# GpSimd forms the low words of four weight slots of each expert pass in place of two

## The chip, the cores and the metric

The kernel runs on one core of one Trainium2 chip. The metric is the device time in microseconds (us) of one execution; smaller is better.

## The reference

One decoder layer on 1024 tokens of width 1024: a mixer (recurrent branch, sliding-window attention, cross-attention into 256 memory tokens, output projection, residual), then a mixture of experts. The mixer is untouched here. The part that the change lies in is this, cut down:

```python
logits = xt @ w_router + b_router                 # 1024 tokens, 32 experts
top_vals, top_idx = lax.top_k(logits, 4)
gates = softmax(top_vals)
# for each expert, on the tokens that chose it:
h = x_tokens @ w1[e] + b1[e]                      # 1024 -> 2048
x_glu = minimum(h[..., ::2], 7);  x_lin = clip(h[..., 1::2], -7, 7)
a = x_glu * sigmoid(1.702 * x_glu) * (x_lin + 1)
out[tokens] += (a @ w2[e] + b2[e]) * gate         # 1024 -> 1024
```

## The kernel before

All is float32. A matmul takes its operands in a rounded form, so each operand is split into a high word (the rounded value) and a low word (the value minus the high word), and a product is made of three matmuls, high by high, high by low, low by high (`three`, L1030 to L1032).

The experts run in *passes* (a hardware loop, one program for each engine). A pass is one expert on up to 256 tokens, in one or two groups of 128; I call passes with one group single and with two groups double. The weights of a pass come in 12 *slots* of 1 MB: 0 to 7 hold the first matrix (two slots for each of four quarters j of the hidden width), 8 to 11 the second. For every slot:

- SyncE loads it into `ring` (6 places). A load waits until the low words of the slot six before it are made, and these waits stand in slot order.
- ScalarE makes the high words `w_hi` (L712) into one of 4 places (`SPLIT`). It waits until TensorE has used the slot four before (`w_used`).
- VectorE, or for the slots in `BY_POOL` GpSimd, makes the low words `w_lo` = `ring` - `w_hi` (VectorE L1461, a helper that also makes `xT_lo` and `actT_lo`; GpSimd L501), and tells TensorE and SyncE by a semaphore (`lo_ready` for VectorE, `lo_pool` for GpSimd).
- TensorE uses it: 12 matmuls of 128x512 for each group.

The order of an engine's work in a pass is written out by hand. VectorE runs `split_lo(3)`, `split_lo(4)`, then for j = 0 to 3: `add_bias(j)` (for each group `hb` L1524 from PSUM, `glu` L1530, `lin` L1531, and `lin` L1535), for j = 0 the index of the next pass (`make_idx`, L1455 and L1457, which waits for GpSimd's `idx_cur` L505), `split_lo(2j+5)`, for j = 3 `take_xlo` (`xT_lo` of the next pass's group 0), `times_sigmoid(j)` (`act` L1544), for j > 0 `take_alo(j-1)` (`actT_lo`), `split_lo(2j+6)`, and for j = 1 `make_onehot` (L1449). Slots 12, 13, 14 are slots 0, 1, 2 of the next pass. `split_lo` returns at once for a slot in `BY_POOL`. After the four quarters come `take_alo(3)`, slots 13 and 14, `combine` and the `xT_lo` of group 1.

ScalarE runs `split_hi(3)`, `split_hi(4)`, and then for each j: `split_hi(2j+5)`, `sigmoid(j)` (L721), for j = 3 `take_xhi` (`xT_hi`, L687), for j > 0 `take_ahi(j-1)` (`actT_hi`, L727), `split_hi(2j+6)`. `add_bias(j)` waits for TensorE to be done with slot 2j+1.

GpSimd runs in each pass: copy `idx_cur`, two indirect DMAs `xg` (L480) that fetch the next pass's tokens, one DMA `rows` (L514) for each group that fetches the rows of `out`, then the low words of its slots in order, then one DMA `out` (L522) for each group that writes the rows back; at the pass's end it waits for these to land before the next pass's `idx_cur`.

TensorE's slot 9 writes the PSUM bank in which the transposed tokens of the next pass lie, so `down(9)` waits for `xT_lo` of group 0 (`xlo_ready`).

Of the kernel before, what the change touches and what calls it, by code (L numbers as in the profile page):

```python
# [50 lines left out]
RAW = 6  # L51
SPLIT = 4
LEAD = 3
BY_POOL = (7, 11)
AHEAD_OOB = 1 << 20


# [12 lines left out]
def hymba_layer(nc, x, mem, g_mix, w_in, conv_w, conv_b, lru_wa, lru_ba, lru_wx, lru_bx, lru_lambda,  # L70
# [3 lines left out]
    with ExitStack() as ctx:  # L74
# [199 lines left out]
        def split_before(s, by_pool):  # L274

            return sum((i % NSLOT in BY_POOL) == by_pool for i in range(s + 1))

# [22 lines left out]
        def _(sp):  # L300
# [57 lines left out]
            with sp.Fori(0, total) as p:  # L358
# [3 lines left out]

                sp.reg_mul(split_reg, p, NSLOT - len(BY_POOL))
                sp.reg_mul(pool_reg, p, len(BY_POOL))
                for s in range(RAW, RAW + NSLOT):

                    if (s - RAW) % NSLOT in BY_POOL:
                        sp.reg_add(pool_reg, pool_reg, 1)
# [16 lines left out]
        def _(po):  # L385
# [105 lines left out]
            with po.Fori(0, total) as p:  # L491
# [6 lines left out]
                def body(groups):  # L498
                    def split_lo(s):
                        po.wait_ge(hi_ready, p12 + (s + 1))  # L500
                        po.tensor_tensor(w_lo[s % SPLIT][:, :, :], slot(s), w_hi[s % SPLIT][:, :, :].bitcast(F32),  # L501
                                         ALU.subtract).then_inc(lo_pool, 1)
# [9 lines left out]
                    for g in groups:  # L512
# [3 lines left out]
                                              bounds_check=last_row, oob_is_err=False).then_inc(rows_in[g], 16)  # L516
                    for s in BY_POOL:
                        split_lo(s)
# [234 lines left out]
        def _(pe):  # L753
# [285 lines left out]
            with pe.Fori(0, total) as p:  # L1039
                two = pe.value_load(ttab[0:1, bass.ds(p + TTWO, 1)], min_val=0, max_val=1)  # L1040
                dbl = pe.value_load(ttab[0:1, bass.ds(p + TDBL, 1)], min_val=0, max_val=NPASS)
                p_dve, p_pool = pe.snap(p * (NSLOT - len(BY_POOL))), pe.snap(p * len(BY_POOL))

# [578 lines left out]
```

## Time and profile before

| what | us |
|---|---|
| device time, median of 3 runs | 2646.74 (2640.09 to 2650.44) |
| span of the profiled execution, first to last instruction | 2640.5 |
| TensorE matmul busy | 2244.2 (85%) |
| VectorE busy | 1864.1 (71%) |
| ScalarE busy | 1157.0 (44%) |
| GpSimd busy | 638.1 (24%) |

The profiled execution's device time is not listed apart from its span; the span lies 6.2 us under the median of the runs and within their spread. The mixer and the routing take the first 638 us of the span, the 32 passes the rest. The shares are means over all of it. The passes are of few kinds, and passes of one kind are alike, so the change is read in one pass of a kind, in order of time, and multiplied.

### The profile page before, as it was taken

Reading aid. Unit: us, or ns where it says so; the run is one execution under the profiler, and the core shown is the slowest. Engines: PE = TensorE matmul, PEld = TensorE weight load, DVE = VectorE, ACT = ScalarE, POOL = GpSimd, SP = SyncE. Lnnn points to the kernel's source line nnn. Section 1 sums busy time; section 2 is a strip of 40 time slices with the busy share of each in tenths; the row PEclk is TensorE's granted clock in tenths of the full one; section 3 lists DMA queues with packets and bytes.
Section 4 is the critical chain, followed back from the end, with each engine's and each line's share of the span. In section 5 each row is a group of like instructions: output and inputs, shape, how many; then the busy total and the mean of one; then the engine's idle time right before and its main releaser. Section 6 shows DMA issues by size and latency. Waiting matters only on the chain.

```text
span 2640.5 us, 31740 instructions
## 1 busy us (share of the span) xinstructions
PE 2244.2 (85%) x9880; PEld 1699.7 (64%) x9881; DVE 1864.1 (71%) x2162; ACT 1157.0 (44%) x1253; POOL 638.1 (24%) x309
## 2 busy tenths in 40 slices
PE   6998788987699867987798989896777998998996
PEld 4453576444577755766676767675566786786784
DVE  4023773337887887888778888888787778778777
ACT  3025341113444544455444545454554445445444
POOL 1002000002222232223323232323223223223222
PEclk9998997987999977988898989998888998998998
DMA  6001001006776677667767676767777667667665
GB/s 220 0 1 64 25 1 72 32 26 245 268 250 221 230 257 277 232 241 255 267 221 274 226 271 230 245 235 250 265 244 263 219 216 281 216 206 276 215 206 200
DMA packets 244998, 524.29 MB, mean 199 GB/s; under 512 B 17576, under 2 KB 22760, under 8 KB 240737
## 3 DMA queue, kind: packets, MB, share of 16 engines
q1 hardware_dynamic: 220990, 467.84, 50.8%
q0 software_dynamic: 23904, 55.95, 5.6%
q8 instruction: 23, 0.38, 0.1%
q14 instruction: 15, 0.11, 0.0%
q10 hardware_dynamic: 66, 0.02, 0.0%
HBM read 522.20 MB, written 32.11 MB: 210 GB/s over the span
## 4 chain that ended last, share of the span: by engine, by line
PE 45%; DVE 20%; issue 11%; DMA 3%; DVEq 3%; ACT 2%; POOLq 0%; POOL 0%; ACTq 0%
PE ps L1030 12%; PE ps L1032 12%; PE ps L1031 12%; DVE w_lo L1461 5%; PE ps L955 5%; DVE glu L1530 3%; DMA out<-rows,idx_cur 3%; DVE lin L1531 3%; DVE hb L1524 2%; DVE onehot L1449 2%; DVE xT_lo L1461 2%; DVE lin L1535 1%; PE ps L1065 1%; ACT w_hi L712 1%; ACT xT_hi L687 1%
## 5 line engine op out<-in xcount | busy, mean ns | idle before, releaser
L712 ACT ACTIVATE w_hi<-ring 128x2048 fp32r<-128x2048 f32 x384 | 731.2, 1914 | 365.8 <-PE ps L1032 365.5
L1461 DVE TENSOR_TENSOR w_lo<-ring,w_hi 128x2048 fp32r<-128x2048 f32 x323 | 736.5, 2285 | 97.7 <-ACT w_hi L712 93.3
L1030 PE MATMUL ps<-w_hi,xT_hi 128*128 128x512 f32 x1440 | 585.7, 407 | 6.9 <-DVE xT_lo L1461 6.9
L1032 PE MATMUL ps<-w_hi,xT_lo 128*128 128x512 f32 x1440 | 574.8, 399 | 0.0
L1031 PE MATMUL ps<-w_lo,xT_hi 128*128 128x512 f32 x1440 | 574.7, 399 | 0.0
L1030 PE MATMUL ps<-w_hi,actT_hi 128*128 128x512 f32 x720 | 321.5, 447 | 203.6 <-DVE xT_lo L1461 159.8
L501 POOL TENSOR_TENSOR w_lo<-ring,w_hi 128x2048 fp32r<-128x2048 f32 x64 | 316.6, 4947 | 445.6 <-ACT w_hi L712 445.1
L1030 PEld LDWEIGHTS ps<-w_hi,xT_hi 128*128 128x128 f32 x1440 | 280.2, 195 | 63.4 <-issue 7.1
L1032 PEld LDWEIGHTS ps<-w_hi,xT_lo 128*128 128x128 f32 x1440 | 278.6, 193 | 61.4
L1031 PEld LDWEIGHTS ps<-w_lo,xT_hi 128*128 128x128 f32 x1440 | 279.8, 194 | 56.9
L1030 PEld LDWEIGHTS ps<-w_hi,actT_hi 128*128 128x128 f32 x720 | 150.0, 208 | 250.3 <-DVE xT_lo L1461 168.6
L1032 PE MATMUL ps<-w_hi,actT_lo 128*128 128x512 f32 x720 | 305.5, 424 | 0.0
L1031 PE MATMUL ps<-w_lo,actT_hi 128*128 128x512 f32 x720 | 304.4, 423 | 0.0
L522 POOL DMA_INDIRECT out<-rows,idx_cur x45 | 82.2, 1826 | 650.2 <-DVE rows L1561 644.8
L721 ACT ACTIVATE sig<-glu 128x256 f32<-128x256 f32 x180 | 72.7, 414 | 366.4 <-DVE glu L1530 366.1
L727 ACT ACTIVATE actT_hi<-ps 128x256 fp32r<-128x256 f32 x180 | 62.8, 379 | 274.0 <-PE ps L1065 274.0
L1032 PEld LDWEIGHTS ps<-w_hi,actT_lo 128*128 128x128 f32 x720 | 148.8, 207 | 35.3
L1031 PEld LDWEIGHTS ps<-w_lo,actT_hi 128*128 128x128 f32 x720 | 150.7, 209 | 28.3
L1531 DVE TENSOR_SCALAR lin<-hb 128x256 f32<-128x256 f32 x180 | 166.4, 925 | 0.0
L1544 DVE TENSOR_TENSOR act<-lin,sig 128x256 f32<-128x256 f32 x180 | 164.5, 937 | 2.0
L1524 DVE TENSOR_TENSOR hb<-ps,b1b 128x512 f32<-128x512 f32 x180 | 123.1, 684 | 49.4 <-PE ps L1032 49.4
L480 POOL DMA_INDIRECT xg<-token_rows,idx_next x66 | 124.9, 1892 | 105.2 <-issue 79.7
(260 smaller groups left out, 2356.9 us busy)
## 6 DMA issues: line engine op xcount, KB each, us to landing
ring<-in_w SPq DMA_DIRECT2D x390, 1024.0 KB, 5.1
b1b<-in_b SPq DMA_DIRECT2D x33, 1024.0 KB, 6.7
xh<-in_x SPq DMA_DIRECT2D x2, 2048.0 KB, 17.3
work<-in_w_out SPq DMA_DIRECT2D x1, 4096.0 KB, 12.8
token_rows<-uT POOLq DMA_DIRECT2D x8, 512.0 KB, 2.9
out<-xh SPq DMA_DIRECT2D x8, 512.0 KB, 2.6
work<-in_w_in SPq DMA_DIRECT2D x2, 1536.0 KB, 19.8
uT<-in_w_mem_kv SPq DMA_DIRECT2D x1, 2048.0 KB, 17.5
```

What stands on the lines that cost most here:

```text
L480: po.indirect_dma_start(out=xg[:, g, :], out_offset=None, in_=xrows[:, :], in_offset=by_index(idx_next, g), bounds_check=last_row, oob_is_ ...
L501: po.tensor_tensor(w_lo[s % SPLIT][:, :, :], slot(s), w_hi[s % SPLIT][:, :, :].bitcast(F32), ALU.subtract).then_inc(lo_pool, 1)
L522: po.indirect_dma_start(out=out[0], out_offset=by_index(idx_cur, g), in_=rows[:, g, :], in_offset=None, bounds_check=last_row, oob_is_err= ...
L712: act_e.activation(w_hi[s % SPLIT][:, :, :], slot(s), ACT.Copy).then_inc(hi_ready, 1)
L955: m = pe.matmul(ps[:, 2 * g + half, :], uT[:, c, i * P:(i + 1) * P], w_out_sb[:, kk + n, half * HALF:(half + 1) * HALF], start=n == 0, sto ...
L1030: pe.matmul(acc, hi, whi, start=first, stop=False)
L1031: pe.matmul(acc, hi, wlo, start=False, stop=False)
L1032: return pe.matmul(acc, lo, whi, start=False, stop=last)
L1461: return dve.tensor_tensor(lo, x, hi.bitcast(F32), ALU.subtract)
L1524: dve.tensor_tensor(hj, ps[:, 2 * (j % 2) + g, :], b1b[:, j * HALF:(j + 1) * HALF], ALU.add).then_inc(h_free[g], 1)
L1531: dve.tensor_scalar(lin[:, g, j % 2, :], pair[:, 1, :], LIMIT, -LIMIT, ALU.min, ALU.max).then_inc(lin_ready[g], 1)
L1544: dve.tensor_tensor(act[:, g, j % 2, :], lin[:, g, j % 2, :], sig[:, g, j % 2, :], ALU.mult).then_inc(act_ready[g], 1)
```

## The change

`BY_POOL` goes from two slots to four. From it follow, without other edits, the slots that `split_lo` of VectorE skips, the loop of GpSimd, the counts that TensorE and SyncE wait for on the two semaphores (`p * len(BY_POOL)`, `p * (NSLOT - len(BY_POOL))`), and which semaphore each waits on for slots 5 and 9.

```diff
-BY_POOL = (7, 11)
+BY_POOL = (5, 7, 9, 11)
```

## Rows read from the trace of the kernel before

**Rows 1.** Windows, three passes: us; busy (x) PE, PEld, DVE, ACT, POOL; PEclk, DMA, GB/s.

```profile
1379.66:1432.29 52.63, 41.04 (x171) 32.69 (x171) 46.08 (x43) 29.01 (x24) 16.51 (x7) 0.87 0.79 283
1248.20:1306.20 58.00, 42.62 (x171) 33.83 (x171) 46.12 (x42) 29.05 (x24) 18.81 (x7) 0.85 0.75 267
1432.29:1505.80 73.51, 71.63 (x352) 58.83 (x351) 56.30 (x69) 32.96 (x33) 20.16 (x10) 0.98 0.64 221
```

**Rows 2.** Timeline of TensorE at slot 9, in the first single and the double pass.

```profile
1416.82 0.79 PE L1030 MATMUL ps<-w_hi,actT_hi 128*128 128x512 f32 x1 [7.46 <-DVE xT_lo L1461]
...
1483.01 0.50 PE L1030 MATMUL ps<-w_hi,actT_hi 128*128 128x512 f32 x1 [1.88 <-DVE xT_lo L1461]
```

**Rows 3.** Timeline of VectorE in the first single pass, start and duration in us.

```profile
1392.87 5.37 DVE L1544 TENSOR_TENSOR act<-lin,sig 128x256 f32<-128x256 f32 x1
...
1407.36 2.28 DVE L1461 TENSOR_TENSOR w_lo<-ring,w_hi 128x2048 fp32r<-128x2048 f32 x1
1409.56 0.68 DVE L1524 TENSOR_TENSOR hb<-ps,b1b 128x512 f32<-128x512 f32 x1
1410.28 3.87 DVE L1530 TENSOR_SCALAR glu<-hb 128x256 f32<-128x256 f32 x1
...
1415.54 1.23 DVE L1461 TENSOR_TENSOR xT_lo<-ps,xT_hi 128x1024 fp32r<-128x1024 f32 x1 [0.73 <-ACT xT_hi L687]
```

**Rows 4.** Groups by line: count, busy us, mean ns of one, idle before.

```profile
L1461 DVE TENSOR_TENSOR w_lo<-ring,w_hi 128x2048 fp32r<-128x2048 f32 x323 | 736.5, 2285 | 97.7 <-ACT w_hi L712 93.3 <-issue 3.9
L712 ACT ACTIVATE w_hi<-ring 128x2048 fp32r<-128x2048 f32 x384 | 731.2, 1914 | 365.8 <-PE ps L1032 365.5
L501 POOL TENSOR_TENSOR w_lo<-ring,w_hi 128x2048 fp32r<-128x2048 f32 x64 | 316.6, 4947 | 445.6 <-ACT w_hi L712 445.1
L1531 DVE TENSOR_SCALAR lin<-hb 128x256 f32<-128x256 f32 x180 | 166.4, 925 | 0.0
L1544 DVE TENSOR_TENSOR act<-lin,sig 128x256 f32<-128x256 f32 x180 | 164.5, 937 | 2.0
L1530 DVE TENSOR_SCALAR glu<-hb 128x256 f32<-128x256 f32 x180 | 122.1, 678 | 6.2
L721 ACT ACTIVATE sig<-glu 128x256 f32<-128x256 f32 x180 | 72.7, 414 | 366.4 <-DVE glu L1530 366.1
L727 ACT ACTIVATE actT_hi<-ps 128x256 fp32r<-128x256 f32 x180 | 62.8, 379 | 274.0 <-PE ps L1065 274.0
L514 POOL DMA_INDIRECT rows<-out,idx_cur x45 | 61.7, 1370 | 13.7 <-issue 13.7
```

**Rows 5.** Single lines, whole span: duration ns min/median/max, first and last start.

```profile
L501 POOL TENSOR_TENSOR w_lo<-ring,w_hi x64: 4584/4648/5706, 655.6 to 2606.4; 128x2048 fp32r<-128x2048 f32 x64
...
L1544 DVE TENSOR_TENSOR act<-lin,sig x180: 408/418/5380, 650.6 to 2614.8; 128x256 f32<-128x256 f32 x180
...
L1531 DVE TENSOR_SCALAR lin<-hb x180: 273/286/4734, 647.4 to 2612.1; 128x256 f32<-128x256 f32 x180
...
L1530 DVE TENSOR_SCALAR glu<-hb x180: 293/295/3887, 647.2 to 2608.3; 128x256 f32<-128x256 f32 x180
```

**Rows 6.** Timeline of GpSimd in the first single pass.

```profile
1392.31 0.99 POOL L514 DMA_INDIRECT rows<-out,idx_cur  x1 [0.30 <-issue]
1393.32 4.63 POOL L501 TENSOR_TENSOR w_lo<-ring,w_hi 128x2048 fp32r<-128x2048 f32 x1
1408.30 5.69 POOL L501 TENSOR_TENSOR w_lo<-ring,w_hi 128x2048 fp32r<-128x2048 f32 x1 [10.35 <-ACT w_hi L712]
```

**Rows 7.** Windows over slot 9, single and double pass.

```profile
1416.82:1422.38 5.56, 5.56 (x14) 4.29 (x15) 2.90 (x3) 0.76 (x1) 0.00 (x0) 0.50 0.93 344
1483.01:1490.56 7.55, 7.55 (x29) 6.07 (x29) 3.47 (x5) 0.39 (x1) 0.00 (x0) 0.77 0.98 378
```

**Rows 8.** Timeline of GpSimd and VectorE in the double pass.

```profile
1451.59 0.99 POOL L514 DMA_INDIRECT rows<-out,idx_cur  x1 [0.30 <-issue]
1453.62 4.67 POOL L501 TENSOR_TENSOR w_lo<-ring,w_hi 128x2048 fp32r<-128x2048 f32 x1 [1.04 <-ACT w_hi L712]
1476.36 4.64 POOL L501 TENSOR_TENSOR w_lo<-ring,w_hi 128x2048 fp32r<-128x2048 f32 x1 [18.06 <-ACT w_hi L712]
...
1453.71 4.73 DVE L1531 TENSOR_SCALAR lin<-hb 128x256 f32<-128x256 f32 x1
```

## The prediction

> **What bounds the kernel now.** I read first the windows over single passes, then the waits inside them, then the durations that don't fit their own median. A single pass takes 52.6 us behind a double pass and 58.0 us behind a single one, a double pass 73.5 us; VectorE is busy 46.1 us of a single pass and TensorE 41.0 us; in a double pass it is 56.3 and 71.6 us [rows 1]. So a double pass is nearly TensorE's, a single pass nearly VectorE's. What TensorE waits for last in both is the same: slot 9 waits for `xT_lo` of the next pass's tokens, 7.46 us in the single and 1.88 us in the double pass [rows 2]. Behind slot 9 no wait on weights is left that the change touches. The question is therefore: when does VectorE end `xT_lo` (now 1415.54 + 1.23 = 1416.77) [rows 3]?
>
> VectorE's busy time is not all work. The three small operations `act`, `lin` and `glu` have medians of 418, 286 and 295 ns but means of 937, 925 and 678 [rows 4, 5]. The excess, 180 x (519 + 639 + 383) ns = 277 us, is nearly GpSimd's whole time on low words, 316.6 us [rows 4]. In order of time one sees why: `act`, ready at 1392.87, ends at 1398.24, with GpSimd's operation from 1393.32 to 1397.95; `glu` at 1410.28 ends at 1414.15, GpSimd at 1413.99 [rows 3, 6]. It holds the other way too: the second GpSimd operation was issued at 1408.30, inside VectorE's `w_lo` of 1407.36 to 1409.64, and took 5.69 us in place of the median 4.65, the 1.04 us being the wait [rows 3, 5, 6]. Only `hb`, which reads PSUM, ran beside it (1409.56, its usual 0.68) [rows 3]. So the two engines exclude each other while GpSimd makes low words, and VectorE's operations on SBUF stand still.
>
> **What the change does, part by part.** The loop has 384 / 12 = 32 passes and 45 groups, so 13 double and 19 single [rows 4].
>
> Slots 5 and 9 leave VectorE: two operations of 2.285 us [rows 4], 2.2 each since neighbours overlap by 0.08. They come to GpSimd at 4.65 each [rows 5]. GpSimd is idle when they come, but the exclusion charges them to VectorE. I walk the single pass at 1379.66.
>
> (a) *Slot 5.* GpSimd's order puts it behind its DMA issues, the last of which ends at 1393.30 [rows 6]. VectorE's own slot 5 no longer stands against these issues; I take 0.9 us for that (bounds 0, and 2.2, the whole operation): start 1392.4. Slot 7 follows at once, as its high words are old. The `act` above was ready before GpSimd's `w_lo` was issued but behind a DMA issue that had begun at 1392.31 [rows 3, 6], and lost: an instruction that follows directly keeps the port. So VectorE stands until 1392.4 + 2 x 4.65 = 1401.7, where it was free of this at 1398.24. `act` and `actT_lo` (0.75) are now done before. Slot 8 on VectorE starts at 1401.7, where it was 1398.24 + 0.3 = 1398.5: +3.2. TensorE's slot 5 starts at 1397.1, where no wait was; with slots 5, 6 and 7 (12 matmuls each, 5.2 us for the first at the clock of [rows 7], some 3 for the others) it ends slot 7 near 1408.6. That is ahead of the port's chain, so I cost the late slot 5 itself at nothing; if the chain were shorter than some 5 us more, this would take over.
>
> The Trainium skill ("SBUF — State Buffer", section "Who interferes with whom") says that a VectorE instruction with two SBUF inputs, or in a two-port mode, contends with a GpSimd instruction that reads SBUF, and that whoever issues first has the port for that one instruction. By that reading the waiting slot 8 would get in between slots 5 and 7; the rows above show the follower winning. Either order leaves the same sum on the port, and the end is the same within 0.5 us.
>
> (b) *Slot 9.* VectorE, slot 8 and `onehot`: 1406.1. The high words of slot 9 wait for TensorE's slot 5 (1402.3) and take 1.9 [rows 4]: 1404.2. GpSimd runs 1406.1 to 1410.8, beside it only `hb` (0.65). So 4.65 - 2.2 - 0.65 = +1.8.
>
> (c) *ScalarE's order.* The high words of slot 10 are queued behind `sig` and `actT_hi`, and `sig` needs the `glu` that GpSimd has just held up: 0.3 + 0.41 + 0.38 + 1.91 [rows 4, 5] after 1410.8 is 1413.8, while VectorE has 1.7 us of work: +1.4. Today they are ready before VectorE asks.
>
> (d) *Slot 11* waits behind VectorE's slot 10 and covers `hb` as today; 1407.36 to 1416.77 is 9.4 us [rows 3] and stays. `xT_lo` ends at 1413.9 + 9.4 = 1423.3: +6.5 for a single pass (3.2 + 1.8 + 1.4 is 6.4). In single passes behind a single one GpSimd comes 5.4 us later as today (52.6 against 58.0) [rows 1]; TensorE then idles longer ahead of slot 5, but the port chain starts from the same GpSimd issue, so I take 6.5 too.
>
> *Double pass.* GpSimd was free at 1452.58 and waited 1.04 us for high words [rows 8]. Slot 5's are old, so it starts at 1451.6 to 1452.6, and slot 7 follows. VectorE stood from 1453.71 to 1458.44 [rows 8], behind one and a half groups of `add_bias`; now it stands from about 1452.3 to 1460.9 with that work still ahead: +4.1. High words of slot 8 behind the late `sig`: +1.1. Slot 9: +1.8. Slot 10's high words: +1.1. Slot 11 (1476.36) [rows 8] came after 2.84 us of waiting and of `add_bias(3)`; now it comes at once, and what it pushes back costs 2.15: -0.7. Sum 7.4, by the walk 7.7; I take 7.6. TensorE's slot 5 was due at about 1457.2 and gets its words at 1456.3 to 1457.2: nothing, cover under 1 us. Slot 9 after a longer idle runs longer at the granted clock 0.50 (1.2 GHz), as the single pass shows; 7.55 us at 0.77 [rows 7] could lose 1 us more: I take 0.5. So +8.1.
>
> Loads: SyncE's load of slot 11 now waits for GpSimd's slot 5 (1397.1), with those of the next slots 0 and 1 behind it in order. Slot 11 is wanted at about 1415.8 and slot 12 later still; VectorE's own late slots are later than that queue. Nothing, with 15 us of cover.
>
> Sum: 19 x 6.5 + 13 x 8.1 = 123.5 + 105.3 = 228.8 us. Span 2640.5 + 228.8 = 2869.3; with the 6.2 us by which the median stands above the span, 2876.
>
> **Bounds.** Low: no wait for ScalarE and more covered, 3.0 + 1.5 = 4.5 us in each pass, 144 us: 2791. High: nothing covered, 2 x 4.65 = 9.3 less some early time of slot 5, 9 us: 288 us, 2935.
>
> **The rivals.**
> 1. *Relief.* VectorE loses 4.4 us of work a pass and GpSimd's operations fall on time in which VectorE waits anyway. Place: slot 9's, ahead of `xT_lo`. Price: 2.2 us gained a pass, 70 us, 2576. It decides from the point where GpSimd's stretch lies in VectorE's idle time, as it would if it ran behind `xT_lo`. Against: 277 of 316.6 us were not so [rows 4, 5], and VectorE is idle only 6.5 us of a single pass [rows 1]. "Perfetto Trace Analysis" of the Trainium skill ("Optimizing Scalar/DVE Operations") says that moving work between these two might not help; by that the time would be 2647 or above. 3 in 100.
> 2. *TensorE's double passes take it up.* 71.6 of 73.5 us are TensorE's, and slot 9 has but 1.88 us of waiting. If VectorE's 17.2 us of slack in such a pass took up all but 1 us, 19 x 6.5 + 13 = 136: 2783. Against: slot 9 waits on the very chain. 8 in 100.
> 3. *The port is shared more finely,* or ScalarE's waits don't arise: 4.5 to 5 a pass, 2791 to 2807. 17 in 100.
> 4. *Starvation.* GpSimd's operations also push `onehot` and slot 10, and TensorE's slot 8 waits at the low clock: 9 a pass or more, 2935 and above. 10 in 100.
> 5. *It doesn't do what it says.* All counts come from `BY_POOL`; were it so, 2647. 2 in 100.
>
> **How the numbers follow.** My forecast has 60 in 100: 2876. The range takes in the bounds and rival 3 and the edge of 4: 2790 to 2935. About 0.5% is what a measurement of this kernel can tell from no change; faster by more 0.03, within 0.02, slower 0.95.
>
> **What would show it.** The GpSimd group at 128 operations of 4.6 to 5.7 us; the excess of `act`, `lin`, `glu`, `onehot` or `w_lo` over their medians grown by some 250 us; VectorE busy nearly as before or more despite 64 operations fewer; TensorE waiting for GpSimd ahead of slot 5 in single passes; slot 9's wait for `xT_lo` near 7 us in double passes; passes of 59, 64.5 and 81.5 us. It is wrong if the excess stays at 277 us, or if double passes stay under 76 us.

## The result and the profile after

The changed kernel takes 2850.86 us (median of 4 runs, 2849.45 to 2860.49) against 2643.41 us for the kernel before (4 runs): a ratio of 1.0792, 95% interval 1.0765 to 1.0818. It is slower by 207 us. The prediction said 2876, so +229 us from the profiled span.

The profiled execution of the changed kernel spans 2858.8 us. Of the 218.3 us over before's span, 5.7 lie ahead of the first pass, which the change doesn't touch, and 212.6 in the 32 passes. First the busy times, then the same kinds of windows as in [rows 1]: a single pass behind a double one, a single behind a single, a double one.

```profile
PE 2269.6 (79%) x9880; PEld 1719.1 (60%) x9881; DVE 1983.0 (69%) x2098; ACT 1154.4 (40%) x1253; POOL 911.7 (32%) x373
```

```profile
1464.01:1521.63 57.62, 42.01 (x171) 33.48 (x171) 50.04 (x40) 29.10 (x24) 25.66 (x9) 0.85 0.73 258
1320.20:1383.70 63.50, 41.28 (x171) 32.76 (x171) 49.67 (x40) 29.15 (x24) 28.06 (x9) 0.84 0.70 244
1521.63:1601.20 79.57, 71.89 (x351) 58.78 (x351) 59.32 (x67) 32.69 (x33) 28.36 (x12) 0.96 0.60 204
```

VectorE has 64 instructions fewer and is busy 119 us longer. The groups by line tell where (count, busy us, mean ns of one, idle before; those of before are in [rows 4]):

```profile
L1461 DVE TENSOR_TENSOR w_lo<-ring,w_hi 128x2048 fp32r<-128x2048 f32 x259 | 671.1, 2598 | 181.3 <-ACT w_hi L712 177.1 <-issue 3.9
L501 POOL TENSOR_TENSOR w_lo<-ring,w_hi 128x2048 fp32r<-128x2048 f32 x128 | 620.6, 4861 | 350.0 <-ACT w_hi L712 349.3
L1530 DVE TENSOR_SCALAR glu<-hb 128x256 f32<-128x256 f32 x180 | 334.4, 1858 | 6.2
L1449 DVE TENSOR_TENSOR onehot<-iota_s,vm 128x2048 f16 x34 | 161.3, 4744 | 2.9 <-issue 2.9
L1544 DVE TENSOR_TENSOR act<-lin,sig 128x256 f32<-128x256 f32 x180 | 155.6, 888 | 6.6 <-ACT sig L721 2.4
L1531 DVE TENSOR_SCALAR lin<-hb 128x256 f32<-128x256 f32 x180 | 50.9, 283 | 0.0
```

Over durations of 0.295, 0.418 and 2.28 us, `glu` stands still for 281 us, `act` for 85, `onehot` for 84 and `w_lo` for some 81 us: 531 us together, where before it was 277. (Before, `onehot` and `w_lo` took their own 2.28 us.) That is 0.86 of GpSimd's 620.6 us on low words, where it was 0.88 of 316.6 before. In order of time, GpSimd and then VectorE in the first of the three windows:

```profile
1475.79 0.99 POOL L514 DMA_INDIRECT rows<-out,idx_cur  x1 [0.30 <-issue]
1476.80 9.04 POOL L501 TENSOR_TENSOR w_lo<-ring,w_hi 128x2048 fp32r<-128x2048 f32 x2
1488.79 6.53 POOL L501 TENSOR_TENSOR w_lo<-ring,w_hi 128x2048 fp32r<-128x2048 f32 x1 [2.95 <-ACT w_hi L712]
1499.87 4.80 POOL L501 TENSOR_TENSOR w_lo<-ring,w_hi 128x2048 fp32r<-128x2048 f32 x1 [4.55 <-ACT w_hi L712]
```

```profile
1476.35 9.78 DVE L1544 TENSOR_TENSOR act<-lin,sig 128x256 f32<-128x256 f32 x1
...
1491.50 3.97 DVE L1530 TENSOR_SCALAR glu<-hb 128x256 f32<-128x256 f32 x1
...
1498.02 2.29 DVE L1461 TENSOR_TENSOR w_lo<-ring,w_hi 128x2048 fp32r<-128x2048 f32 x1 [1.04 <-ACT w_hi L712]
1500.23 0.68 DVE L1524 TENSOR_TENSOR hb<-ps,b1b 128x512 f32<-128x512 f32 x1
1500.95 3.87 DVE L1530 TENSOR_SCALAR glu<-hb 128x256 f32<-128x256 f32 x1
...
1506.21 1.23 DVE L1461 TENSOR_TENSOR xT_lo<-ps,xT_hi 128x1024 fp32r<-128x1024 f32 x1 [0.73 <-ACT xT_hi L687]
```

One `act` of 0.42 us takes 9.78 us: it stands through slots 5 and 7, which GpSimd does one behind the other. `glu` stands through slot 9, VectorE waits 1.04 us for the high words of slot 10, and `glu` stands through slot 11. TensorE's waits over the whole span:

```profile
PE ps L1030 <- DVE xT_lo L1461: 246.7, 33, 8.6
PE ps L1030 <- POOL w_lo L501: 148.7, 19, 9.8
PE ps L1030 <- DVE actT_lo L1461: 42.1, 26, 2.5
```

The second is new: slot 5's low words, in each of the 19 single passes. The first grew from 166.7 us, most of it in double passes, where the wait ahead of slot 9 is now 6.7 us and was 1.9. So two causes stand side by side in this profile, and the profile alone doesn't say which of them costs the time: VectorE standing still (exclusion), or TensorE getting its weights from a slower engine (lateness). The experiments are made for that.

### The profile page after: what moved, and what is told of

Read it like the earlier page. It is cut to its first block, busy times and chain, and to the rows that moved or that the text cites. A ratio compares the mean times of both kernels' runs of the same rounds, so it can differ in the third digit from the quotient of the medians.

```text
span 2858.8 us, 31740 instructions
## 1 busy us (share of the span) xinstructions
PE 2269.6 (79%) x9880; PEld 1719.1 (60%) x9881; DVE 1983.0 (69%) x2098; ACT 1154.4 (40%) x1253; POOL 911.7 (32%) x373
## 4 chain that ended last, share of the span: by engine, by line
PE 33%; issue 20%; DVE 19%; ACT 8%; DMA 3%; DVEq 2%; POOLq 0%; ACTq 0%; POOL 0%
PE ps L1030 9%; PE ps L1031 8%; PE ps L1032 8%; DVE onehot L1449 6%; DVE glu L1530 5%; ACT w_hi L712 5%; PE ps L955 4%; DVE hb L1524 3%; DMA out<-rows,idx_cur 3%; DVE xT_lo L1461 1%; DVE w_lo L1461 1%; ACT xT_hi L687 1%; ACT actT_hi L727 1%; DVEq L1448 1%; PE ps L1024 1%
## 5 line engine op out<-in xcount | busy, mean ns | idle before, releaser
L1461 DVE TENSOR_TENSOR w_lo<-ring,w_hi 128x2048 fp32r<-128x2048 f32 x259 | 671.1, 2598 | 181.3 <-ACT w_hi L712 177.1
L501 POOL TENSOR_TENSOR w_lo<-ring,w_hi 128x2048 fp32r<-128x2048 f32 x128 | 620.6, 4861 | 350.0 <-ACT w_hi L712 349.3
L1030 PE MATMUL ps<-w_hi,xT_hi 128*128 128x512 f32 x1440 | 588.6, 409 | 155.6 <-POOL w_lo L501 148.7
L1030 PE MATMUL ps<-w_hi,actT_hi 128*128 128x512 f32 x720 | 331.2, 460 | 303.1 <-DVE xT_lo L1461 239.8
L1530 DVE TENSOR_SCALAR glu<-hb 128x256 f32<-128x256 f32 x180 | 334.4, 1858 | 6.2
L1031 PE MATMUL ps<-w_lo,actT_hi 128*128 128x512 f32 x720 | 311.9, 433 | 0.0
L1449 DVE TENSOR_TENSOR onehot<-iota_s,vm 128x2048 f16 x34 | 161.3, 4744 | 2.9 <-issue 2.9
L1544 DVE TENSOR_TENSOR act<-lin,sig 128x256 f32<-128x256 f32 x180 | 155.6, 888 | 6.6 <-ACT sig L721 2.4
L1461 DVE TENSOR_TENSOR actT_lo<-ps,actT_hi 128x256 fp32r<-128x256 f32 x180 | 70.7, 417 | 116.1 <-ACT actT_hi L727 116.1
## 6 DMA issues: line engine op xcount, KB each, us to landing
work<-in_w_out SPq DMA_DIRECT2D x1, 4096.0 KB, 12.8
```

The costliest lines, as they stand in the source:

```text
L1030: pe.matmul(acc, hi, whi, start=first, stop=False)
L1031: pe.matmul(acc, hi, wlo, start=False, stop=False)
L1449: dve.tensor_tensor(onehot[:, :, :], iota_s[:, bass.ds(part * PASS, PASS)].rearrange("p (a s) -> p a s", a=1).to_broadcast([P, NT, PASS]), ...
L1461: return dve.tensor_tensor(lo, x, hi.bitcast(F32), ALU.subtract)
L1530: dve.tensor_scalar(glu[:, g, j % 2, :], pair[:, 0, :], LIMIT, None, ALU.min).then_inc(glu_ready[g], 1)
L1544: dve.tensor_tensor(act[:, g, j % 2, :], lin[:, g, j % 2, :], sig[:, g, j % 2, :], ALU.mult).then_inc(act_ready[g], 1)
```

## The experiments

All ratios are against the kernel before on the same chip (2640 us, medians of 7 runs; each experiment is the median of 4). The means by kind of pass that I give are from the profiles, before's being 52.4 us for a single pass behind a double one, 57.6 behind a single one, and 72.8 for a double one.

**One slot at a time.**

```diff
-BY_POOL = (7, 11)
+BY_POOL = (7, 9, 11)
```

> The kernel before with slot 9 alone added to GpSimd's (7, 9, 11). Exclusion (GpSimd's 4.65 us on SBUF stop VectorE, only the PSUM-reading hb runs beside): 4.65 less 2.2 less 0.65 = 1.8 us a pass, and 1.1 to 1.4 for the high words of slot 10 behind the late sigmoid: some +3.1 us a pass, +100 us, 2745. Lateness (TensorE waits for words that the slower engine makes later): slot 9's words are old when TensorE comes to it, so nothing: 2643. The wait for GpSimd ahead of slot 5 doesn't appear by either.

Measured: 2752.30 us, ratio 1.0421 (1.0404 to 1.0439): +112.

```diff
-BY_POOL = (7, 11)
+BY_POOL = (5, 7, 11)
```

> The kernel before with slot 5 alone added (5, 7, 11). Exclusion: +3.2 us in single passes, +4 to +5 in double ones (slot 8's high words behind the late sigmoid too), some +120 us: 2765. Lateness: all of the change's 207 us, as TensorE waits 6 to 10 us for slot 5 in single passes: 2850, and double passes as before. Both: slot 5 starts near 17.3 us into a single pass behind a double one.

Measured: 2765.59 us, ratio 1.0467 (1.0447 to 1.0486): +125. The wait for GpSimd ahead of slot 5 is the same as in the changed kernel, to the tenth:

```profile
PE ps L1030 <- DVE xT_lo L1461: 214.9, 33, 7.5
PE ps L1030 <- POOL w_lo L501: 148.7, 19, 9.8
```

Lateness as the cause of all of it falls with both: slot 9, whose words TensorE doesn't wait for, costs nearly as much as slot 5, and slot 5 with its 148.7 us of waiting costs 125 and not 207. The two sum to 237, 30 us more than both together.

**Late, without reading SBUF.** VectorE makes slots 5 and 9 as before; GpSimd is kept busy in their place, for some 7.3 us a stretch where the low words take 4.85, and TensorE waits for it. The stand-in only writes, but for six small operations that read two elements of each operand per partition. (The semaphore `beside` and a first memset of the tile, ahead of the passes, are left out below.)

```diff
-                    for s in BY_POOL:
-                        split_lo(s)
+                    def stand_in(n):
+                        for i in range(6):
+                            po.wait_ge(beside, pb + (12 * n + 2 * i + 1))
+                            po.tensor_tensor(scratch[:, 510:512], iota_s[:, 0:2], iota_s[:, 2:4], ALU.subtract).then_inc(beside, 1)
+                            po.memset(scratch[:, 0:510], 0.0).then_inc(beside, 1)
+
+                    for s in (5, 7, 9, 11):
+                        if s in BY_POOL:
+                            split_lo(s)
+                        else:
+                            po.wait_ge(hi_ready, p12 + (s + 1))
+                            stand_in((s - 5) // 4)
...
                 def wait_split(s):
+                    if s in (5, 9):
+                        pe.wait_ge(beside, pb + (12 * ((s - 5) // 4 + 1) + 1))
```

> The kernel before (7, 11), where GpSimd, at the places in its order where the changed kernel makes the low words of slots 5 and 9, does about as long a stretch of small memsets (with five two-element operations between them) into a tile that nobody reads, and TensorE waits for its end ahead of slots 5 and 9. VectorE still makes these slots' words. So TensorE gets slots 5 and 9 as late as in the changed kernel, but GpSimd reads next to nothing from SBUF. Lateness: 2850, like the changed kernel. Exclusion: slot 5 late by 6 to 8 us, slot 7 done at 29 to 35 us into a single pass, just when VectorE comes to need it: 0 to +40 us, 2643 to 2683. If memsets exclude VectorE too, glu and lin at least grow beyond before's 0.68 and 0.93 us.

Measured: 2671.30 us, ratio 1.0123 (1.0101 to 1.0144): +31. TensorE's longest wait is now for GpSimd, longer than in the changed kernel, and the loss is 31 us (the stand-in writes the tile `km`; its wait is at L1045):

```profile
PE ps L1045 <- POOL km L526: 212.1, 32, 11.8
PE ps L1045 <- DVE xT_lo L1480: 92.9, 33, 6.9
```

As these waits grew, TensorE's waits for `xT_lo`, `actT_lo` and `act`, 276.2 us in the kernel before, come to 104.3. The 31 us are not the price of lateness alone, as the stand-in also moves GpSimd's slot 7; the next pair of runs parts the two.

**The same without TensorE's wait, and with reads in place of memsets.**

```diff
-                    def stand_in(n): ...six small memsets, as above
+                    def stand_in(n):
+                        for i in range(4):
+                            po.wait_ge(beside, pb + (4 * n + i + 1))
+                            po.tensor_tensor(scratch, iota_s[:, 0:512], iota_s[:, 512:1024], ALU.subtract).then_inc(beside, 1)
```

> The kernel before (7, 11), VectorE making slots 5 and 9 as ever, and at the places in GpSimd's order where the changed kernel has slots 5 and 9, four subtractions of 128x512 on SBUF into a tile that nobody reads. TensorE and SyncE wait for nothing new. Exclusion: some 4.7 us of standing still for each such stretch and no work taken off VectorE: +9 us a pass, 2850 to 2940, so as slow as the changed kernel or slower, with glu, act, lin or w_lo far over their medians. Lateness: no weight comes later through a wait on GpSimd apart from slots 7 and 11, so 2643 to 2660.

> The same with the small memsets of late_only in place of the subtractions, and no wait of TensorE for them. Exclusion by reads: 2643 to 2671 (late_only had 2671 with TensorE's waits on top). If any GpSimd work of that length did it, as read_beside, 2850 or more.

Measured: 2867.49 us with reads, ratio 1.0862 (1.0844 to 1.0880), and 2622.95 us with memsets, 0.9935 (0.9918 to 0.9951). So added GpSimd work whose result nobody waits for makes the kernel as slow as the changed one if it reads SBUF, and no slower at all if it mostly writes. Both stand-ins delay slot 7, which GpSimd still makes, and TensorE waits for that; but the wait is the longer one in the fast kernel, so it isn't what makes the other slow. With reads, then with memsets:

```profile
PE ps L1044 <- POOL w_lo L506: 195.2, 19, 10.8
```

```profile
PE ps L1045 <- POOL w_lo L506: 225.1, 19, 12.7
```

The groups with reads (GpSimd's stand-in at L525):

```profile
L1475 DVE TENSOR_TENSOR w_lo<-ring,w_hi 128x2048 fp32r<-128x2048 f32 x323 | 834.9, 2590 | 97.2 <-ACT w_hi L726 92.8 <-issue 3.9
L525 POOL TENSOR_TENSOR km<-iota_s 128x512 f32<-128x512 f32 x256 | 496.0, 1937 | 40.6 <-ACT w_hi L726 24.8
L1558 DVE TENSOR_TENSOR act<-lin,sig 128x256 f32<-128x256 f32 x180 | 180.1, 1024 | 2.0
```

write_beside and late_only differ in TensorE's wait alone: 2622.95 against 2671.30 us. So handing slots 5 and 9 over late costs 48 us there, 1.7 to 1.8 us in a single pass and 0.4 in a double one, and that with longer waits for slot 5 (10.4 and 11.8 us in single passes) than in the changed kernel (6.2 and 9.8).

That write_beside is 17 us faster than before I had not expected. Its single passes behind a single one are 4.6 us shorter, its double ones some 3 us longer; the stand-in pushes GpSimd's slot 7 later. Why that is a gain in the one and a loss in the other I have not tried.

**The other way: nothing on GpSimd, and slot 11 alone.**

```diff
-BY_POOL = (7, 11)
+BY_POOL = ()
```

> GpSimd makes no low words, VectorE all twelve. Exclusion: VectorE does 4.4 us more a pass but loses 9.3 us of standing still, of which 0.65 was covered: single passes 4.5 us shorter, double ones 2 to 3.5 (the wait ahead of slot 9 was 1.9 us, and the lower clock behind it goes too): 2643 - 19 x 4.5 - 13 x 2.8 = 2521. act, lin and glu back at 0.42, 0.29 and 0.30 us on the mean. Relief (VectorE is short of time, and what leaves it helps): slower than before by up to 2 x 2.2 x 32 = 140 us, 2784.

Measured: 2493.62 us, ratio 0.9448 (0.9432 to 0.9464): 147 us faster than before, and Relief is refuted. I had expected 2521: the cost of the two slots was larger than I took it. Single passes are 5.6 us shorter (`xT_lo` ends 5.1 to 5.2 us sooner), double ones 3.1.

```profile
L1461 DVE TENSOR_TENSOR w_lo<-ring,w_hi 128x2048 fp32r<-128x2048 f32 x387 | 883.0, 2286 | 133.2 <-ACT w_hi L712 128.9 <-issue 3.8
L1449 DVE TENSOR_TENSOR onehot<-iota_s,vm 128x2048 f16 x34 | 77.6, 2282 | 2.9 <-issue 2.9
L1544 DVE TENSOR_TENSOR act<-lin,sig 128x256 f32<-128x256 f32 x180 | 70.8, 417 | 0.0
L1530 DVE TENSOR_SCALAR glu<-hb 128x256 f32<-128x256 f32 x180 | 54.0, 300 | 6.2
L1531 DVE TENSOR_SCALAR lin<-hb 128x256 f32<-128x256 f32 x180 | 51.2, 284 | 0.0
```

Every group is at its median. VectorE makes all low words and is busy less, 1728.1 us against 1864.1.

```diff
-BY_POOL = (7, 11)
+BY_POOL = (11,)
```

> Slot 11 alone on GpSimd (11). Exclusion: slot 11's operation blocks VectorE from hb(3) to glu(3), 4.65 less 2.2 less 0.65 of hb = 1.8 us a pass over no_pool (2494), the rest of before's 147 us being slot 7's: 2494 + 32 x 1.8 = 2552. If slot 7 carries all (its operation is covered by nothing), 2494; if both carry the same, 2567.

Measured: 2580.17 us, ratio 0.9772 (0.9744 to 0.9800). Slot 11 costs 87 us over no_pool and slot 7 another 60. I had expected 2552, so my split was wrong, and the passes say why: in double passes `xT_lo` ends at 50.4 to 50.7 us with slot 7 on GpSimd or without it. Without it VectorE waits 1.3 us for the high words of slot 8 and 0.4 us for those of slot 10, and with it not at all; slot 7's standing still falls on these waits. In single passes `xT_lo` ends 2.2 to 2.4 us later by slot 11 and 2.9 by slot 7. Slot 11 has no such cover: double passes are 3.2 us longer by it.

**Where it reaches TensorE.** `xT_lo` of group 0 is taken ahead of `add_bias(3)`, and its high words ahead of slot 11's.

```diff
-                        split_hi(2 * j + 5)
-                        sigmoid(j)
                         if j == 3:
                             take_xhi(x2 + 1, 0)
+                        split_hi(2 * j + 5)
+                        sigmoid(j)
...
+                        if j == 3:
+                            take_xlo(x2 + 1, 0)
                         add_bias(j)
...
                         split_lo(2 * j + 5)
-                        if j == 3:
-                            take_xlo(x2 + 1, 0)
```

> The changed kernel (5, 7, 9, 11) with xT_lo of the next pass's group 0 taken ahead of add_bias(3) on VectorE, and its high words ahead of split_hi(11) on ScalarE. xT_lo reads PSUM and one SBUF operand. If slot 9's wait for xT_lo is where VectorE's standing still reaches the end, xT_lo now ends right behind slot 10's low words, 38 us into a single pass in place of 44, and in double passes 49 in place of 56.6: 4 to 6 us a pass, 2851 - 32 x 5 = 2690. If the time is lost elsewhere (slot 5, the late high words), 2830 to 2851.

> no_pool with the same two moves. xT_lo at 28.3 us into a single pass in place of 32.0; the wait ahead of slot 9 was 4.5 to 5 us in single passes and nothing in double ones: 19 x 3 to 4 us and a little clock, 2494 - 65 = 2430. If VectorE's later add_bias(3) costs as much behind slot 9: 2494.

> The kernel before (7, 11) with the two moves of early_x. With none of the slots on GpSimd it was 2404, with four 2690. If each GpSimd operation still takes about as much from VectorE wherever xT_lo stands, this lies about half way, 2530 to 2560. If only what stands ahead of slot 9 counted, slot 11, which now lies behind xT_lo, would be free, and slot 7 alone would be paid: 2404 + 32 x 2.7 = 2490.

Measured: 2689.69 us with four slots on GpSimd, ratio 1.0182 (1.0162 to 1.0201); 2404.11 with none, 0.9101 (0.9083 to 0.9118); 2494.87 with two, 0.9443 (0.9415 to 0.9470). The four-slot kernel lies where expected; with none the gain was larger than expected (2430). With four, the two moves give back 161 us, and TensorE's waits for `xT_lo` shrink from 246.7 us to:

```profile
PE ps L1030 <- DVE xT_lo L1461: 33.4, 20, 6.9
```

But the moves also gain 145 us with two slots and 90 with none. So the step from two slots to four costs 195 us in this order too, against 207. It falls otherwise: double passes pay 3.1 us for it in place of 7.5, single passes 7.7 to 7.8 in place of 5.5 to 6.2. In double passes, then, the larger part of the standing still reached TensorE through `xT_lo`. In single passes, where VectorE is busy 50 of 56 us with four slots and 45 of 48 with two, it costs no less when `xT_lo` is out of its way. By which waits is not separated; TensorE's wait for slot 5 is still there in this order (116.2 us in sum), and its price in it is open.

With two, the single pass whose first instruction starts at 1313.83 shows how slot 11 runs now; GpSimd, then VectorE:

```profile
1343.37 4.88 POOL L501 TENSOR_TENSOR w_lo<-ring,w_hi 128x2048 fp32r<-128x2048 f32 x1 [11.27 <-ACT w_hi L712]
```

```profile
1343.71 1.22 DVE L1461 TENSOR_TENSOR xT_lo<-ps,xT_hi 128x1024 fp32r<-128x1024 f32 x1
1344.84 0.68 DVE L1524 TENSOR_TENSOR hb<-ps,b1b 128x512 f32<-128x512 f32 x1
1345.55 2.84 DVE L1530 TENSOR_SCALAR glu<-hb 128x256 f32<-128x256 f32 x1
```

`xT_lo` and `hb`, which read PSUM, both run at their own length beside GpSimd, and `glu` stands for 2.5 us in place of 3.6. The total meets the second expectation, but its split doesn't: double passes pay 1.4 us over early_x_none where 2.7 was set, single ones 3.1 to 4.5. So slot 11 isn't shown to be free. How much each slot pays in that order I have not separated.

early_x_none is the fastest kernel here: 9% under the kernel before and 447 us under the changed one. TensorE is busy all through its double passes (69.6 to 69.9 us), and single ones are down from 52.4 and 57.6 to 43.5 and 45.3, of which VectorE is busy 41.7.

## Why the prediction was right, and where it was off

*What bounds it.* Right for the kernel as it was written. `xT_lo` ends 6.3 to 7.1 us later in single passes behind a double one, 5.7 behind a single one, and these passes are 6.2 and 5.5 us longer. It is not the only place where the standing still can reach the end: with `xT_lo` taken early the same step costs 195 us, most of it in single passes. `xT_lo` marked how late VectorE ran in the order as written, and for the sum that was enough.

*Exclusion.* Right, and shown by taking the cause apart: GpSimd reads beside, no weight handed over (read_beside, 2867 us); work of about the same length, hardly a read (write_beside, 2623 us; 6.8 us a stretch against 7.8 in read_beside), and TensorE made to wait for it (late_only, 2671 us); nothing on GpSimd, all groups at their medians (no_pool, 2494 us).

*(a) Slot 5, single pass.* The two operations of GpSimd start 12.8 us into the pass where the walk had 12.7, and `act` ends at 1486.13, 22.1 us in, where it had 22.0. That an operation which follows directly keeps the port is shown: `act` was ready at 1476.35, half a microsecond ahead of slot 5's operation (GpSimd was then at a DMA issue, until 1476.78), and stood through both. The Trainium skill ("SBUF — State Buffer", "Who interferes with whom") gives the shared pair of ports to whoever issues first, for the whole instruction. I had read from it that the waiting instruction would come in between two of GpSimd's; for operations issued back to back it did not. Where each of GpSimd's operations first waits for the one before it (read_beside), the two engines do alternate. Slot 5's own lateness I costed at nothing. No run takes it out of the changed kernel. read_beside is as slow without it, and slot5_too, which has all of it, has single passes 3.4 and 2.9 us longer where the walk had 3.2 from the standing still alone; late_only against write_beside puts a price of 1.7 to 1.8 us a single pass on a longer one. So nothing, or little, fits these runs.

*(b) Slot 9.* The walk had 1.8 us. slot9_too shows 1.9 for the double passes' `xT_lo` alone and 3.6 for (b) and (c) in single ones, where the walk had 3.2. I had written that the order of `onehot` and slot 9 matters within 0.5 us; here it was a step of 0.7 us. With `onehot` first (the window above, slot 9's words taking 6.53 us) `xT_lo` ends 43.4 us into the pass; where GpSimd came first, in others of its kind, at 44.2.

*(c) ScalarE's order.* Walk 1.4 us, measured 1.04 in the profile above.

*Single passes in sum.* Behind a double pass 6.2 us against 6.5; behind a single one 5.5. I had priced the second kind by the first, and that was the coarser step. The first pass paid 9.4, and with it the 19 come to 115 us against 123.5.

*Double passes.* This term was mis-sized: 7.5 us measured, 8.1 forecast. `xT_lo` ends 5.9 to 6.3 us later in ten of the 13, where the walk had 7.6; in the other three GpSimd comes to slot 5 20.2 us into the pass in place of 18.8 to 19.1, `glu` takes 9.65 us, and `xT_lo` ends 7.3 to 7.4 us later. The standing of `glu` and the waits for ScalarE in one of the ten:

```profile
1541.51 8.34 DVE L1530 TENSOR_SCALAR glu<-hb 128x256 f32<-128x256 f32 x1
...
1553.81 2.29 DVE L1461 TENSOR_TENSOR w_lo<-ring,w_hi 128x2048 fp32r<-128x2048 f32 x1 [0.63 <-ACT w_hi L712]
1556.02 6.69 DVE L1449 TENSOR_TENSOR onehot<-iota_s,vm 128x2048 f16 x1
...
1567.60 2.29 DVE L1461 TENSOR_TENSOR w_lo<-ring,w_hi 128x2048 fp32r<-128x2048 f32 x1 [0.62 <-ACT w_hi L712]
```

Both waits are 0.6 us, where I had set 1.1. `glu` ends at 1549.85, 28.2 us into the pass, where the walk put the end of the standing at 28.6; VectorE comes to slot 8's wait 3.5 us later than in the kernel before, where I had 4.1. These make up 1.6 of the 1.7 us by which this pass's `xT_lo` (5.9 later) stays under the walk. Slot 9 cost 2.2 us here and not 1.8 (`onehot` stood for 4.41 us, and no `hb` ran beside), and less behind slot 10 makes that good.

The longer wait ahead of slot 9 did come (6.7 us in this pass, "near 7"), and what stands behind it at the lower granted clock was more than I took: over the 13 double passes slot 9 takes 7.9 us on the mean (7.1 to 8.6) where it took 6.7 (5.7 to 7.4), so 1.1 us and not 0.5. With the mean of `xT_lo`, 6.4 us later, that makes up the 7.5. So the total was near in part because two errors in this term go against each other: the walk was 1.2 us too long, and the slower slot 9 was taken 0.6 us too short.

Summed, the passes are 212.6 us longer against 228.8, and the median, whose offset to the span I had taken from before, moved by 207.

*The rivals.* Relief has the wrong sign, by no_pool. TensorE's double passes did not take it up: they pay more than the single ones. Finer sharing, at 4.5 to 5 us a pass, and starvation, at 9, enclose the 6.6 us that a pass paid on the mean; neither happened. The late slot 5, which I held to be covered, I can bound only by analogy: its like, with longer waits, cost 48 us (late_only over write_beside).

*The signs that I had named.* 128 operations on GpSimd, at 4.50 to 6.67 us (6.67 is beyond my 5.7: it waited for all of `onehot`); the standing grown by 254 us where I said 250; TensorE waiting for GpSimd ahead of slot 5 in all single passes; passes of 58.6, 63.1 and 80.3 us where I said 59, 64.5 and 81.5.

## What to carry to other kernels

Before work goes from VectorE to an idle GpSimd, look for VectorE operations whose mean is far above their median while GpSimd runs, and price the move as GpSimd's duration less VectorE's, not as a gain of VectorE's. In this kernel an operation of GpSimd that takes twice as long on SBUF would pay only where VectorE has nothing to do but wait, or has PSUM-reading work in its order just there; of the four slots only slot 7 was covered so, in double passes. And where one wait bounds a pass, ask what stands ahead of it in the queue without need: moving `xT_lo` forward was worth 90 us more on top of taking the low words back. Such a move doesn't show by itself where a cost came from: it gained 161, 145 and 90 us with four, two and no slots on GpSimd, and the test is what the change costs in the new order (195 us, against 207).

## What the runs showed of the hardware that I had not expected

- VectorE's `act` stood for 9.78 us through two operations of GpSimd issued back to back, having been ready ahead of the first; against subtractions that each wait for the one before, VectorE got in between (four of 128x512 took 9.3 us in one pass of read_beside, for VectorE's operations in between).
- GpSimd's low words took 4.50 us at the least in the changed kernel, where the least was 4.58 before, and a duration can hold GpSimd's own waiting: of the 4.91 us of slot 9 in the double pass above, 0.45 lie beside the end of VectorE's slot 8, and `onehot` was delayed by 4.41.
- TensorE waited 212 us for GpSimd in late_only, which is 31 us slower than before, and 225 us (for slot 7) in write_beside, which is 17 us faster: the longest entry in its list of waits is no measure of what it costs, as other waits shrank with it.
- A stretch of memsets on GpSimd beside the kernel before made it 0.65% faster (0.9935, 0.9918 to 0.9951). It delays slot 7 on GpSimd; the cause is open.
